# A layer trunk on one Trainium2 core: a small fold matrix in a tile of its own, and the scores of two heads issued alternately on the two row halves of the PE array

## What is computed

```python
mod = (c_act @ w_ada[l] + b_ada[l]).reshape(bsz, 3, 3, D_MODEL)   # shifts, scales, gates
...
# dilated mixer: 12 heads of 64, in 3 groups of 4 (dilation 1, 4, 16)
s = jnp.einsum('brhnid,brhnjd->brhnij', qb, kb) * d ** -0.5
s = jnp.where(valid, s + bias, NEG_BIG)
m = jnp.max(s, axis=-1, keepdims=True)
p = jnp.exp(s - m)
den = jnp.sum(p, axis=-1, keepdims=True)
o = jnp.einsum('brhnij,brhnjd->brhnid', p, vb) / den
```

## Time and profile before

| | us |
|---|---|
| median of three runs | 2841.58 |
| the profiled execution | 2843.08 |
| its span (first to last instruction) | 2841.3 |
| PE busy in the span | 2776.7 (98%) |
| DVE busy | 1614.7 (57%) |
| ACT busy | 1053.2 (37%) |
| mean granted clock of PE, share of full speed | 0.993 |

### The profile page before, as it was taken

How to read it: one execution, slowest core, us unless ns; L and a number is a source line. 1 busy time by engine, 2 the same in 40 slices (tenths; PEclk the granted TensorE clock), 3 DMA queues, 4 the chain that set the end, 5 groups by cost and what they waited for, 6 DMA issues and landing times.

```text
span 2841.3 us, 36046 instructions
## 1 busy us (share of the span) xinstructions
PE 2776.7 (98%) x14501; PEld 2353.0 (83%) x14501; DVE 1614.7 (57%) x2448; ACT 1053.2 (37%) x1586; POOL 62.8 (2%) x54
## 2 busy tenths in 40 slices
PE   7999999999999999999999999999999999999998
PEld 6888888888888888888888888988888887888887
DVE  5766347787455457643276662688855545653323
ACT  4222145555422443222252222554553233522213
POOL 0000000000000110000000000000000002000000
PEclk8999999999999999999999999999999999999999
DMA  7665332222122244542336652322221232443321
GB/s 260 208 193 192 135 90 82 67 68 75 45 60 90 89 136 152 187 134 90 119 119 187 198 193 91 97 75 67 68 60 45 74 101 79 126 142 103 93 101 60
DMA packets 358854, 323.12 MB, mean 114 GB/s; under 512 B 12316, under 2 KB 305696, under 8 KB 357920
## 3 DMA queue, kind: packets, MB, share of 16 engines
q1 hardware_dynamic: 357152, 318.65, 35.9%
q10 hardware_dynamic: 1536, 2.16, 0.3%
HBM read 312.31 MB, written 6.29 MB: 112 GB/s over the span
## 4 chain that ended last, share of the span: by engine, by line
PE 88%; DVE 5%; ACT 3%; issue 2%; POOL 1%; DVEq 0%; POOLq 0%; ACTq 0%
PE PS L855 26%; PE PS L857 25%; PE PS L856 25%; PE PS L1087 2%; PE PS L1173 1%; PE PS L1150 1%; PE PS L1136 1%; PE PS L1195 1%; PE PS L1159 1%; PE PS L874 1%; ACT WH L1292 1%; PE PS L1181 1%; POOL MA L2273 1%; DVE MA L2226 1%; DVE HL L1677 0%
## 5 line engine op out<-in xcount | busy, mean ns | idle before, releaser
L855 PE MATMUL PS<-HH,WH 128*128 128x512 f32 (+1 forms) x2540 | 990.6, 390 | 25.4 <-DVE HL L1677 15.6
L857 PE MATMUL PS<-HH,WL 128*128 128x512 f32 (+1 forms) x2540 | 963.5, 379 | 0.0
L856 PE MATMUL PS<-HL,WH 128*128 128x512 f32 (+1 forms) x2540 | 962.6, 379 | 0.0
L855 PEld LDWEIGHTS PS<-HH,WH 128*128 128x128 f32 x2540 | 481.3, 189 | 121.2 <-DVE HL L1677 18.3
L1758 DVE TENSOR_TENSOR WL<-RAW,WH 128x2048 fp32r<-128x2048 f32 x142 | 325.5, 2292 | 423.3 <-ACT WH L1292 423.3
L857 PEld LDWEIGHTS PS<-HH,WL 128*128 128x128 f32 x2540 | 480.9, 189 | 90.9
L856 PEld LDWEIGHTS PS<-HL,WH 128*128 128x128 f32 x2540 | 481.9, 190 | 85.2 <-issue 2.9
L1292 ACT ACTIVATE WH<-RAW 128x2048 fp32r<-128x2048 f32 x142 | 271.8, 1914 | 679.6 <-PE PS L857 661.1
L856 PE MATMUL PS<-GL,WH 128*128 128x512 f32 (+1 forms) x696 | 258.9, 372 | 0.0
L855 PE MATMUL PS<-GH,WH 128*128 128x512 f32 (+1 forms) x696 | 258.9, 372 | 0.0
L857 PE MATMUL PS<-GH,WL 128*128 128x512 f32 (+1 forms) x696 | 258.8, 372 | 0.0
(11 more groups left out here) (262 smaller groups left out, 3443.5 us busy)
## 6 DMA issues: line engine op xcount, KB each, us to landing
RAW<-in_ffn_w_in SPq DMA_DIRECT2D x176, 512.0 KB, 5.2
RAW<-in_w_in SPq DMA_DIRECT2D x132, 512.0 KB, 4.8
AW<-in_w_ada SPq DMA_DIRECT2D x248, 256.0 KB, 4.5
RAW<-in_ffn_w_out SPq DMA_DIRECT2D x88, 512.0 KB, 4.3
AWB<-in_w_ada SPq DMA_DIRECT2D x4, 2048.0 KB, 14.6
RAW<-in_w_out SPq DMA_DIRECT2D x16, 512.0 KB, 4.0
x_kept<-X SPq DMA_DIRECT2D x2, 2048.0 KB, 6.3
X<-x_kept SPq DMA_DIRECT2D x2, 2048.0 KB, 9.4
```

The lines of the kernel that those rows point to most:

```text
L855: pe.matmul(o, ah, bh, start=start, stop=skip, skip_group_check=skip)
L856: pe.matmul(o, ah, bl, start=False, stop=skip, skip_group_check=skip)
L857: return pe.matmul(o, al, bh, start=False, stop=stop or skip, skip_group_check=skip)
```

## The change

- `fold` becomes the last block of the constants, and gets a tile `FOLD` with a DMA of its own in the first block (after `LMF`). `CT` is 512 bytes a partition shorter; its first load is 256 columns wide and not 384. DVE's wait for `LMF`, and a new wait of PE ahead of the first fold matmul, take in that DMA.
- The small tables and `FOLD` move behind the phase region; `phase` lies 3072 bytes lower.
- The units of a pair come head by head in turn: (head 0, tile 0), (head 1, tile 0), (head 0, tile 2), (head 1, tile 2). `c_scores` is called at even slots alone and makes the scores of units n and n + 1: eight matmuls that alternate between the partitions 0 to 63 with bank 2 and the partitions 64 to 127 with bank 3. It waits for the bias of unit n - 1, where before it waited for that of n - 2.

```diff
-for _name, _n in (("ident", P), ("ones", P), ("fold", P), ("ntri", P), ("nones", P), ("negm", P), ("strict", P),
-                  ("reset", SEQ), ("del0", TT * 2 * P), ("del1", P), ("del2", P)):
+for _name, _n in (("ident", P), ("ones", P), ("ntri", P), ("nones", P), ("negm", P), ("strict", P),
+                  ("reset", SEQ), ("del0", TT * 2 * P), ("del1", P), ("del2", P), ("fold", P)):
...
+NHELD = NCONST - P
...
-    CT = sb("CT", [P, NCONST])
+    CT = sb("CT", [P, NHELD])
+    phase = at[0]
...
+    at[0] = phase + 100992
     LM = sb("LM", [P, A_LEVELS, P // 2], U8)
...
+    FOLD = sb("FOLD", [P, P])
     ALATE = sb("ALATE", [P, ADA_LATE * 16])
-    phase = at[0]
...
-    units = [(h, i) for h in range(C_HEADS) for i in ((0, 2) if h < C_SLOTS else (0,))]
+    units = [(2 * p + e, i) for p in range(C_HEADS // 2) for i in ((0, 2) if 2 * p < C_SLOTS else (0,)) for e in range(2)]
...
-            sp.dma_start(CT[:, 0:3 * P], t["const_f"][:, 0:3 * P]).then_inc(const_in, 16)
+            sp.dma_start(CT[:, 0:2 * P], t["const_f"][:, 0:2 * P]).then_inc(const_in, 16)
...
             sp.dma_start(LMF[:, :], t["const_m"]).then_inc(lmf_in, 16)
+            sp.dma_start(FOLD[:, :], t["const_f"][:, NHELD:]).then_inc(lmf_in, 16)
...
-            dve.wait_ge(lmf_in, 16)
+            dve.wait_ge(lmf_in, 32)
...
+                    if part == 0:
+                        pe.wait_ge(lmf_in, 32)
                     pe.wait_ge(ada_folded, at(ada_folded, ADA_BEFORE[part // 2] + i0 + count))
-                    pe.matmul(PS[:, bank, 0:16 * count], const("fold"), src[:, 0:16 * count],
+                    pe.matmul(PS[:, bank, 0:16 * count], FOLD[:, :], src[:, 0:16 * count],
                               start=True, stop=True).then_inc(ada_sum, 1)
...
                 def c_scores(n):
-                    h, t0 = units[n]
-                    pair, pr = h // 2, slice((h % 2) * HD, (h % 2) * HD + HD)
+
+                    pair, t0 = units[n][0] // 2, units[n][1]
                     pe.wait_ge(*taken(TILE0[ITEM_C + pair] + 1))
                     if n == 0:
                         pe.wait_ge(b_out, at(b_out, B_HEADS))
-                    pe.wait_ge(c_bias, at(c_bias, max(n - 1, 0)))
+                    pe.wait_ge(c_bias, at(c_bias, n))
                     for q in range(4):
-                        tq, tk = (t0 + q // 2, max(t0 + q // 2 - 1 + q % 2, 0)) if h < C_SLOTS else (q, q)
-                        mm = pe.matmul(PS[:, 2 + n % 2, q * P:(q + 1) * P], CQ[pair % 2][pr, tq * P:(tq + 1) * P],
-                                       CK[pair % 2][pr, tk * P:(tk + 1) * P], start=True, stop=True)
-                    mm.then_inc(c_s, 1)
+                        for e in range(2):
+                            pr = slice(e * HD, e * HD + HD)
+                            tq, tk = (t0 + q // 2, max(t0 + q // 2 - 1 + q % 2, 0)) if 2 * pair < C_SLOTS else (q, q)
+                            mm = pe.matmul(PS[:, 2 + e, q * P:(q + 1) * P], CQ[pair % 2][pr, tq * P:(tq + 1) * P],
+                                           CK[pair % 2][pr, tk * P:(tk + 1) * P], start=True, stop=True)
+                            if q == 3:
+                                mm.then_inc(c_s, 1)
...
-                        if n < NU:
+                        if n < NU and n % 2 == 0:
                             c_scores(n)
```

More of the change, by code:

```diff
@@ L249, in body, with const @@
     CT_AT = at[0]
-    CT = sb("CT", [P, NCONST])
+    CT = sb("CT", [P, NHELD])
+    phase = at[0]
+    def const(name):
+        a, n = CONST[name]
+        return CT[:, a:a + n]
+    ident, ones = const("ident"), const("ones")
+    GH = sb("GH", [P, FT, SEQ], F32R, phase)
+    GL = sb("GL", [P, FT, SEQ], F32R, phase + FT * 2048)
+    at[0] = phase + 2 * FT * 2048
+    SB = [sb(f"SB{i}", [P, SEQ]) for i in range(2)]
+    AW = [sb(f"AW{i}", [P, SEQ]) for i in range(2)]
+    AACC = [sb("AACC0", [P, SEQ])]
+    spare = CT_AT + 4 * 2 * P
+    AW += [sb(f"AW{2 + i}", [P, SEQ], F32, spare + 2048 * i) for i in range(2)]
+    AACC.append(sb("AACC2", [P, SEQ], F32, spare + 4096))
+    ATURN = sb("ATURN", [P, SEQ], F32, spare + 6144)
+    AFOLD = sb("AFOLD", [P, ADA_EARLY * 16], F32, spare + 8192)
+    assert spare + 8192 + 64 * ADA_EARLY <= CT_AT + 4 * NHELD
+    at[0] = phase + 100992
     LM = sb("LM", [P, A_LEVELS, P // 2], U8)
@@ L262, in body @@
     NGR = sb("NGR", [P, A_V])
+    FOLD = sb("FOLD", [P, P])
     ALATE = sb("ALATE", [P, ADA_LATE * 16])
-    phase = at[0]
-    def const(name):
-        a, n = CONST[name]
-        return CT[:, a:a + n]
-    ident, ones = const("ident"), const("ones")
-    GH = sb("GH", [P, FT, SEQ], F32R, phase)
-    GL = sb("GL", [P, FT, SEQ], F32R, phase + FT * 2048)
-    at[0] = phase + 2 * FT * 2048
[L276 to L284, removed]
     AWB = [sb(f"AWB{i}", [P, KT, SEQ], F32, phase + 16384 * i) for i in range(FIRST_WAVE)]
@@ L801, in ffn @@
                         sp.wait_ge(ada_sum, at(ada_sum, 1))
-                        c = 3 * P
-                        sp.dma_start(CT[:, c:], t["const_f"][:, c:]).then_inc(mix_const, 16)
+                        c = 2 * P
+                        sp.dma_start(CT[:, c:], t["const_f"][:, c:NHELD]).then_inc(mix_const, 16)
                     row_groups(g1, name_out, 4, FO)
@@ L1558, in mixers @@
                         act.activation(CR[:, 0, :], ident, ACT.Copy)
-                        act.activation(CR[:, 1:4, :], CT[:, 3 * P:6 * P].rearrange("p (n c) -> p n c", n=3), ACT.Copy).then_inc(c_round, 1)
+                        act.activation(CR[:, 1:4, :], CT[:, 2 * P:5 * P].rearrange("p (n c) -> p n c", n=3), ACT.Copy).then_inc(c_round, 1)
                     hb = 2 * (m - (ITEM_B + 2)) + k // 4
```

## The result

| | before | with the change |
|---|---|---|
| median (us) | 2841.51 (2839.51 to 2842.42, 4 runs) | 2826.72 (2825.46 to 2827.25, 4 runs) |
| span of the profiled execution | 2841.3 | 2825.5 |
| PE busy | 2776.7 | 2758.7 |

The ratio is 0.9948, with a 95% interval from 0.9931 to 0.9965: 14.8 us less, 0.5%. 2827.2 was predicted. Two further series of the changed kernel, each beside runs of the kernel before on its own chip, gave 0.9945 [0.9933, 0.9958] and 0.9948 [0.9932, 0.9963].

The account below looks back on a forecast made before the run. PE was taken to bound the kernel, busy 98% of the span. Scores 17.8 us off, less 3.2 of waits and 0.2 for the extra DMA, made 14.4 off 2841.6: 2827.2 us, own range 2825 to 2831, overall 2825 to 2839.

Parts of the forecast that it names:

- the forecast's own mechanism: In a pair's scores, passes on different row halves overlap, two in the time of one; chance 0.46.
- no overlap: Rival: the halves' score loads or passes go one by one, 0.11 us each; 3.8 us off, 2837.8 us; chance 0.38.
- Term (a): Scores on PE: one way in and out of 64-row matmuls less per pair, 0.34 us each, 5.4 us off.
- Term (b): A pair's 16 score passes, two in the time of one: 1.33 us a pair; with Term (a) 17.8 us off.
- the same within half a microsecond: Claim that pricing the scores' overlap by the skill's 4 ns a tile leaves the sum unchanged within that margin.
- The wait: At slot 3 PE's transposes wait for unit 2's exponential: 1.6 us in each layer, 3.2 us in all.
- PE arrives at: Step putting PE at slot 3's transposes at 791.50, while the exponential still ends at 793.06.
- I count no wait: Slots 4 to 7: PE's added transposes and values there about cover the 1.6 us, so no wait.
- FOLD and addresses: Extra DMA issue on SP costs 0.2 us, between 0 and 0.4; moved addresses nothing, bounds 1 us to both sides.
- sign of being wrong: Units' stretch of a layer not shrinking by 7 us, or time moving outside the mixing stages by over 1 us.
- Draining: Rival: each of 112 changes of the row half in the scores costs PE 0.20 us; 2858.8 us, slower; chance 0.10.

Follow-up runs that it names:

- same-rows run: Changed kernel, but in the first two pairs of heads two units of one head alternate between banks on the same 64 rows: 2830.64 us, ratio 0.9958.
- blocks of two: Changed kernel with an even slot's score matmuls ordered a0 a1 b0 b1 a2 a3 b2 b3 (a, b the heads): 2828.09 us, ratio 0.9951.
- head-by-head run: Changed kernel with all four score matmuls of head 0, then all four of head 1, at an even slot: 2833.40 us, ratio 0.9969.
- tables alone: Kernel before with the change's constants, FOLD and addresses but the old scores: 2842.20 us beside 2842.05, ratio 1.0001.
- blocks of three: Changed kernel with an even slot's score matmuls ordered a0 a1 a2 b0 b1 b2 a3 b3 (a, b the heads): 2831.32 us in a single run.

## Why the prediction was right

The time is 0.5 us from the forecast, by the forecast's own mechanism, with two errors that almost cancel. So close a hit is luck; the mechanism is not, though its choice was near to even on record (0.46 against 0.38 for no overlap), since no row of the kernel before had passes that alternate between the halves.

**Term (a), right.** 0.34 us a pair was predicted, and the same-rows run measures 0.336.

**Term (b), the right mechanism, undersized by 1.8 us.** The step that failed: "so the order is a, a, b, b, a, a, b, b, and its first and last pass stay alone: nine steps". They take eight. Head b's first pass does not wait for head a's second one, which stands before it in the program; the first passes of both heads start within 7 ns. A pair's scores now cost 2.577 - 1.341 = 1.236 us and not 1.33, and cost 2 x 1.229 before: 1.22 us saved, 16 x 1.22 = 19.6 us, where 17.8 were predicted. The nine steps of the blocks of two show what the difference is worth: their slots cost 2.679 us against 2.577, 0.10 us a pair and 1.6 us in all, of which the stretches keep 0.9, since PE then waits less. The medians on the same chip, 2828.1 and 2826.4 us, fit this, but the ranges of their runs overlap. The Trainium skill's rule of the prediction ("TensorE: Matmul & The Clock Gate", section "Measured speedup vs the span model", some 4 ns a tile) agrees in kind: 7 ns measured. Taken at its word the rule has two such matmuls last as long as one, which is eight steps; by an estimate from it the forecast's gain would have been 1.5 us larger, less 0.4 us of wait, and not "the same within half a microsecond". The same page's section "The mechanism" has matmuls start and end strictly in program order; the head-by-head run, 13 steps where that order allows at best 15, differs, and the measurement decides.

**The wait, the right place, undersized by 1.1 us.** 1.6 us a layer at slot 3 was predicted. By slot costs with the change, PE loses 0.15 us at slot 1 (0.597 against 0.443 for the same transposes in the same-rows run), 0.38 at slot 2 (2.959 against 2.577), 1.40 at slot 3 (2.739 against 1.341) and 0.21 at slot 7 (1.554 against 1.341): 2.14 us a layer, 4.3 in both, against 3.2. The chain was right: 13.0 us were read from unit 0's bias to the end of unit 2's exponential, and it now runs from 777.61 to 790.61, 13.0 us. The failed step is "PE arrives at": faster scores made PE early at slots 1 and 2 already, where I looked for no wait, and at slot 7, where "I count no wait". The wait at slot 3 is shorter by what PE lost there. By then two pairs' scores were also one step shorter each than counted, 0.2 us in all. The Trainium skill's page "TensorEngine Tiling (Array Packing)" (section "PSUM Bottleneck") has the copying out of PSUM as what may bind once TensorE is faster. The trace agrees in part: PE waits for DVE and ACT in four of a layer's 18 slots, but of the chain above, 5.8 us, only the bias and two copies read PSUM, 1.8 us.

**FOLD and addresses, right within what can be seen.** 0.2 us was predicted; the tables alone cost 0.3 us (between -2.3 and 3.1).

**The sum.** 19.6 - 4.3 = 15.3 us, and the stretches shrank by 15.2. Outside them the two profiles differ by 0.6 us, within the 1 us that I allowed, but that too is luck: it is 2.5 us less in one place and 1.9 us more in another, each above what I had named as a sign of being wrong. Both go with falls of the clock, which come and go from one execution of a kernel to the next: the three profiles of the changed kernel begin their first scores at 776.4, 778.1 and 777.3 us. So the sign was set too narrow for two single executions. Over all runs the mean granted clock is 0.9941 for either kernel, and it has no part in the 14.8 us.

**The rivals.** No overlap would have kept the starts 0.11 us apart and given 2837.8; the same-rows slots are that case. Draining would have shown starts 0.3 us apart: a change of the half cost 7 ns. What spoke for the first, the 0.11 us between loads, was true only of loads that share rows, the objection that stood beside it.

## What to carry to other kernels

Where float32 matmuls with 64 rows come in pairs, put one on each half of the rows, with a bank of its own (whether one bank would do was not tried), and alternate them matmul by matmul: here the second cost 7 ns, and the order matters, since head by head hides three of the eight steps. Then look at who feeds the next step: here the softmax of the second unit was still worked on a slot later, and moving it up took back 1.6 of the 2.1 us that PE waited in each layer. And price each term from its own experiment; a total that fits can hide two errors.

## What the runs showed of the hardware beyond that

- Passes on different halves are started out of program order: four places ahead up to the first pass that runs alone behind a pair, three from there (13 steps head by head, 11 in blocks of three, nine in blocks of two; alternating matmul by matmul, where less reach is needed, eight).
- Loads overlap as the passes do: 16 loads of 64 rows take 0.97 us on two halves, and eight take 0.96 us on one.
- PE's clock was seen at its lower level for some 3 us behind boundaries with a PE gap of 2.6 us in some executions and not in others, worth about 1.7 us each time; a difference of that size between two profiles says nothing about an edit until their clocks are compared.
